# Head statistics by token in 24 columns, preparation reordered, affine parts folded, in the two preparations and two output norms of an RWKV-7 scan

## The reference, cut to what matters

```python
def rwkv7_prepare(pa, prm):
    ...
    decay = jnp.exp(-jnp.exp(-jax.nn.softplus(-w_raw) - 0.5))
    iclr = jax.nn.sigmoid(prm['a0'] + jnp.einsum('bsdl,dlc->bsdc', al, prm['a2']))
    kk = (k * prm['k_k']).reshape(bn, s, A_HEADS_2, HEAD_DIM)
    kk = kk / jnp.maximum(jnp.sqrt(jnp.sum(kk * kk, axis=-1, keepdims=True)), 1e-12)
    k_dir = k[:, :, None, :] * (1 + (iclr - 1) * prm['k_a'])

def rwkv7_output(f, y, prm, dtype):
    mu = jnp.mean(y, axis=-1, keepdims=True)
    var = jnp.mean(jnp.square(y - mu), axis=-1, keepdims=True)
    yn = ((y - mu) * lax.rsqrt(var + GN_EPS)).reshape(bn, s, A_WIDTH_2) * prm['gn_w'] + prm['gn_b']
    bonus = jnp.sum(f['r'][:, :, None] * f['k'] * prm['r_k'], axis=(2, 4))
    yn = yn + (bonus[..., None] * f['v']).reshape(bn, s, A_WIDTH_2)
    return (yn * f['g']).astype(dtype)
```

## Time and profile before

| what | value |
|---|---|
| median of three runs | 3805.64 us (3802.0 to 3807.56) |
| the profiled execution, its time and its span | 3803.02 us, 3801.2 us |
| PE busy in the span | 3201.2 us (84%) |
| DVE busy in the span | 2259.3 us (59%) |
| ACT busy in the span | 1296.1 us (34%) |
| first preparation | 1736.7 to 1785.4 us |
| first output norm | 1972.5 to 1999.1 us |
| second preparation | 1999.1 to 2049.9 us |
| second output norm | 2236.7 to 2264.3 us |

### The profile page before, as it was taken

The page is one execution under the profiler, slowest core; times in us unless marked ns, Lnnn a source line. Parts: engine busy times, 40 slices in busy tenths (PEclk is TensorE's granted clock), DMA queues, the critical chain, the costliest instruction groups (busy, mean ns, idle before and its releaser), DMA issues. The chain is left out here.

```text
span 3801.2 us, 62276 instructions
## 1 busy us (share of the span) xinstructions
PE 3201.2 (84%) x26174; PEld 2598.5 (68%) x26174; DVE 2259.3 (59%) x3957; ACT 1296.1 (34%) x2197; POOL 113.6 (3%) x160
## 2 busy tenths in 40 slices
PE   6679998976999958975765757999999799869998
PEld 5568877644887757843753745888787677657787
DVE  7578876686787566766456455454333546663344
ACT  1233334324333342144323325221233326542233
POOL 0000000200000000000101100000000000000000
PEclk9889999998999979988997988999999898989999
DMA  7235562102334212310000012232212232022231
GB/s 292 99 128 177 171 173 105 68 23 61 123 144 141 87 51 108 125 52 28 5 21 21 4 39 98 89 111 100 78 67 89 78 137 87 1 83 89 89 94 67
DMA packets 64423, 342.37 MB, mean 90 GB/s; under 512 B 15248, under 2 KB 16785, under 8 KB 28433
## 3 DMA queue, kind: packets, MB, share of 16 engines
q1 hardware_dynamic: 61904, 330.75, 25.3%
q0 software_dynamic: 2240, 7.64, 0.6%
HBM read 327.58 MB, written 10.79 MB: 89 GB/s over the span
## 5 line engine op out<-in xcount | busy, mean ns | idle before, releaser
L263 DVE TENSOR_TENSOR weight_lo<-weight_ring,weight_hi 128x1024 fp32r<-128x1024 f32 x341 | 418.7, 1229 | 163.7 <-ACT weight_hi L248 158.4
L248 ACT CAST weight_hi<-weight_ring 128x1024 fp32r<-128x1024 f32 x341 | 355.7, 1043 | 152.6 <-PE banks L418 62.8
L416 PE MATMUL banks<-hT_hi.1,weight_hi 128*128 128x512 f32 x864 | 348.8, 404 | 24.0 <-PEq L380 22.8
L418 PE MATMUL banks<-hT_hi.1,weight_lo 128*128 128x512 f32 x864 | 342.8, 397 | 0.0
L417 PE MATMUL banks<-hT_lo.1,weight_hi 128*128 128x512 f32 x864 | 342.8, 397 | 0.0
L416 PEld LDWEIGHTS banks<-hT_hi.1,weight_hi 128*128 128x128 f32 x864 | 164.3, 190 | 64.2 <-issue 26.0
L417 PEld LDWEIGHTS banks<-hT_lo.1,weight_hi 128*128 128x128 f32 x864 | 164.4, 190 | 38.1 <-issue 1.4
L418 PEld LDWEIGHTS banks<-hT_hi.1,weight_lo 128*128 128x128 f32 x864 | 164.0, 190 | 38.5
L416 PE MATMUL banks<-hT_hi.3,weight_hi 128*128 128x512 f32 (+1 forms) x512 | 175.2, 342 | 7.9 <-PEq L380 7.9
L417 PE MATMUL banks<-hT_lo.3,weight_hi 128*128 128x512 f32 (+1 forms) x512 | 174.1, 340 | 0.0
L418 PE MATMUL banks<-hT_hi.3,weight_lo 128*128 128x512 f32 (+1 forms) x512 | 174.0, 340 | 0.0
(11 more groups left out here) (691 smaller groups left out, 7796.2 us busy)
## 6 DMA issues: line engine op xcount, KB each, us to landing
weight_ring<-ff SPq DMA_DIRECT2D x64, 1024.0 KB, 4.8
weight_ring<-ada SPq DMA_DIRECT2D x48, 1024.0 KB, 4.9
weight_ring<-up SPq DMA_DIRECT2D x44, 1024.0 KB, 4.9
weight_ring<-ada_ffn SPq DMA_DIRECT2D x24, 1024.0 KB, 5.0
weight_ring<-down SPq DMA_DIRECT2D x20, 1024.0 KB, 4.8
first_blocks.1<-ada_mix SPq DMA_DIRECT2D x12, 1024.0 KB, 15.7
weight_ring<-ada_mix SPq DMA_DIRECT2D x12, 1024.0 KB, 4.8
weight_ring<-cv_in SPq DMA_DIRECT2D x8, 1024.0 KB, 4.9
```

The costliest lines, as they stand in the source:

```text
L248: self.nc.scalar.copy(hi, raw).then_inc(self.hi_made, 1)
L263: self.nc.vector.tensor_tensor(lo, raw, hi.bitcast(F32), ALU.subtract).then_inc(self.lo_made, 1)
L416: nc.tensor.matmul(out, w_hi, x_hi, start=first, stop=False)
L418: return nc.tensor.matmul(out, w_lo, x_hi, start=False, stop=last)
```

## The change

It does six things. (1) Sums by head are made by token: the squares are the stationary operand in tiles of 128 tokens, and two columns of `head_ones` the moving one, so that the result is 128 tokens by 2 heads, and all six tiles of both `f` fill 24 columns. (2) Root, maximum and reciprocal work on these 24 columns. (3) `spread_to_features` brings the result back to features: 24 products for each half's pair of tiles, each with one column of the result repeated 64 times as stationary operand and the identity as moving one. `kk`, and `y` in the norm, are multiplied by PSUM directly. (4) The first step of `k_dir` moves from DVE to ACT (an Identity with scale and bias per partition). (5) DVE's order in the preparation changes: the running sums come first with the `k_dir` products between them, then the bonus, then `kk`, the reversal and `iclr*kk`. (6) In the norm the affine part and the sum with the bonus become two `scalar_tensor_tensor`, the second of which also multiplies by the gate, with the shift added after the bonus; one instruction a piece falls away. PE's gate products are cut in two, with the spreading between.

```diff
+    def sums_by_token(to, squares):
+        for t in all_tiles:
+            last = nc.tensor.matmul(to[:, 2 * t:2 * t + 2], squares[:, t * P:(t + 1) * P], head_ones[:, 0:P:HD], start=True, stop=True)
+        return last
+    def spread_to_features(banks, by_token):
+        for t in all_tiles:
+            to = banks[t // 4][:, (t % 4) * P:(t % 4 + 1) * P]
+            for h, part in enumerate((slice(0, HD), slice(HD, P))):
+                last = nc.tensor.matmul(to[part], by_token[:, 2 * t + h:2 * t + h + 1].broadcast_to([P, HD]), ident[:], start=True, stop=True)
+        return last
...
@@ prepare_stage, tensor
-                        for s, seg in enumerate(HALVES):
-                            nc.tensor.matmul(ps[2 * f + s][:, 0:seg.stop - seg.start], head_ones[:], tmp[:, f, seg],
-                                             start=True, stop=True).then_inc(kk_mm, 1)
+                        sums_by_token(ps[7][:, f * 2 * TOK_T:(f + 1) * 2 * TOK_T], tmp[:, f, :]).then_inc(kk_sums, 1)
...
+                    pe.wait_ge(kk_inverse, 1)
+                    for f in range(2):
+                        pe.wait_ge(w_sig, 6 + 2 * f)
+                        spread_to_features(ps[2 * f:2 * f + 2], by_token[:, f, :]).then_inc(kk_spread, 1)
@@ prepare_stage, scalar
-                            nc.scalar.activation(tmp[:, f, seg], ps[2 * f + s][:, 0:seg.stop - seg.start], ACT.Sqrt).then_inc(kk_root, 1)
+                    nc.scalar.activation(by_token[:].rearrange("p f n -> p (f n)"), ps[7][:, 0:4 * TOK_T], ACT.Sqrt).then_inc(kk_root, 1)
...
+                        act.wait_ge(a_sig, 2 * i + 2)
+                        nc.scalar.activation(kdir[:, i, :], iclr[:, i, :], ACT.Identity, bias=omka[:, f0 + f:f0 + f + 1],
+                                             scale=col(R_KA, f0 + f)).then_inc(kdir_begun, 1)
@@ prepare_stage, vector
-                        step(nc.vector.tensor_scalar(tmp[:, f, :], tmp[:, f, :], 1e-12, None, ALU.max))
-                        step(nc.vector.reciprocal(tmp[:, f, :], tmp[:, f, :]))
-                        step(nc.vector.tensor_tensor(kk[:, f, :], kk[:, f, :], tmp[:, f, :], ALU.mult))
...
+                    scan(0)
+                    scan(1)
+                    finish_kdir(0)
+                    scan(2)
+                    finish_kdir(1)
+                    scan(3)
...
+                        dve.wait_ge(kk_spread, f + 1)
+                        for s, seg in enumerate(HALVES):
+                            step(nc.vector.tensor_tensor(kk[:, f, seg], kk[:, f, seg], ps[2 * f + s][:, 0:seg.stop - seg.start], ALU.mult))
@@ head_norm_stage, vector
-                        step(nc.vector.reciprocal(inv[:, f, s], inv[:, f, s]))
-                        step(nc.vector.tensor_tensor(y[:, f, s], y[:, f, s], inv[:, f, s], ALU.mult))
-                        step(nc.vector.tensor_scalar(y[:, f, s], y[:, f, s], rcols[:, R_GW + f0 + f:R_GW + f0 + f + 1],
-                                                     rcols[:, R_GB + f0 + f:R_GB + f0 + f + 1], ALU.mult, ALU.add))
-                        step(nc.vector.tensor_tensor(y[:, f, s], y[:, f, s], mixT[:, f0 + f, s], ALU.add))
+                        dve.wait_ge(spread, f + 1)
+                        step(nc.vector.tensor_tensor(y[:, f, s], y[:, f, s], ps[4 + i][:, 0:n], ALU.mult))
+                        step(nc.vector.scalar_tensor_tensor(out=y[:, f, s], in0=y[:, f, s], scalar=rcols[:, R_GW + f0 + f:R_GW + f0 + f + 1],
+                                                            in1=mixT[:, f0 + f, s], op0=ALU.mult, op1=ALU.add))
                         dve.wait_ge(gate_mm, i + 1)
-                        step(nc.vector.tensor_tensor(mixT[:, f0 + f, s], y[:, f, s], ps[i][:, 0:s.stop - s.start], ALU.mult))
+                        nc.vector.scalar_tensor_tensor(out=mixT[:, f0 + f, s], in0=y[:, f, s], scalar=rcols[:, R_GB + f0 + f:R_GB + f0 + f + 1],
+                                                       in1=ps[i][:, 0:n], op0=ALU.add, op1=ALU.mult)
```

More of the change, by code:

```diff
@@ L2384, in _, with scan @@
                     step = Chain(dve, chained)
[L2385 to L2393 removed]
+                    def scan(i):
                         dve.wait_ge(w_sig, 2 * i + 2)
@@ L2396, in _, with finish_kdir @@
                                                      op0=ALU.mult, op1=ALU.add).then_inc(scanned, 1)
+                    def finish_kdir(i):
+                        dve.wait_ge(kdir_begun, i + 1)
+                        step(nc.vector.tensor_tensor(kdir[:, i, :], kdir[:, i, :], k[:, i % 2, :], ALU.mult))
+                    for f in range(2):
+                        nc.vector.tensor_scalar(kk[:, f, :], k[:, f, :], col(R_KK, f0 + f), None, ALU.mult).then_inc(sq_made, 1)
+                    nc.vector.tensor_scalar(omka[:], rcols[:, R_KA:R_KA + 4], -1.0, 1.0, ALU.mult, ALU.add).then_inc(omka_made, 1)
+                    flat_inverse = by_token[:].rearrange("p f n -> p (f n)")
+                    dve.wait_ge(kk_root, 1)
+                    step(nc.vector.tensor_scalar(flat_inverse, flat_inverse, 1e-12, None, ALU.max))
+                    nc.vector.reciprocal(flat_inverse, flat_inverse).then_inc(kk_inverse, 1)
+                    dve.wait_ge(loaded, 48)
+                    scan(0)
[4 more added lines that the diff above has]
+                    scan(3)
                     dve.wait_ge(scanned, 4)
@@ L2399, in _ @@
                     nc.vector.tensor_copy(gam[:, 1, :, :], chunks[:, :, :, CH]).then_inc(tots, 1)
[L2400 to L2409 removed]
+                    dve.wait_ge(kk_sq, 2)
                     for f in range(2):
+                        finish_kdir(2 + f)
                         step(nc.vector.tensor_tensor(tmp2, kdir[:, f, :], kdir[:, 2 + f, :], ALU.add))
@@ L2864, in _ @@
                         nc.scalar.activation(inv[:, f, s], y[:, f, s], ACT.Square).then_inc(squared, 1)
-                    for i, (f, s) in enumerate(jobs):
-                        act.wait_ge(var_ready, i + 1)
-                        nc.scalar.activation(inv[:, f, s], inv[:, f, s], ACT.Sqrt).then_inc(root_ready, 1)
+                    for f in range(2):
+                        act.wait_ge(var_ready, f + 1)
+                        nc.scalar.activation(by_token[:, f, :], by_token[:, f, :], ACT.Sqrt).then_inc(root_ready, 1)
                 @block.vector
@@ L2875, in _ @@
                                                        op0=ALU.mult, op1=ALU.add).then_inc(centred, 1)
-                    for i, (f, s) in enumerate(jobs):
-                        dve.wait_ge(var_mm, i + 1)
-                        nc.vector.tensor_scalar(inv[:, f, s], ps[4 + i][:, 0:s.stop - s.start], 1.0 / HD, GN_EPS, ALU.mult, ALU.add).then_inc(var_ready, 1)
+                    for f in range(2):
+                        dve.wait_ge(var_sums, f + 1)
+                        nc.vector.tensor_scalar(by_token[:, f, :], ps[6 + f][:, 0:2 * TOK_T], 1.0 / HD, GN_EPS, ALU.mult, ALU.add).then_inc(var_ready, 1)
@@ L2879, in _ @@
+                    for f in range(2):
+                        dve.wait_ge(root_ready, f + 1)
+                        nc.vector.reciprocal(by_token[:, f, :], by_token[:, f, :]).then_inc(inv_ready, 1)
                     dve.wait_ge(centred, 4)
                     for i, (f, s) in enumerate(jobs):
-                        dve.wait_ge(root_ready, i + 1)
-                        step(nc.vector.reciprocal(inv[:, f, s], inv[:, f, s]))
-                        step(nc.vector.tensor_tensor(y[:, f, s], y[:, f, s], inv[:, f, s], ALU.mult))
```

66 lines of the change are left out of this document (35 added, 31 removed).

## The result

The changed kernel takes 3764.71 us, the median of four runs (3763.72 to 3768.02), beside 3803.82 us (3798.84 to 3807.56, four runs) of the kernel before on the same chip. The ratio is 0.9893, with a 95% interval of 0.9881 to 0.9905. The forecast was 3765. The profiled execution took 3763.72 us, with a span of 3761.9.

The account below looks back on a forecast made before the run. DVE was taken to set the end of the four changed stages. Gains of 19.2 (norms), 9.6 and 10.4 us (preparations) take 3803.0 to 3763.8; with the median 2.6 higher, 3765 was written; 8 in 10: 3755 to 3780.

Parts of the forecast that it names:

- The sum: Gain over both preparations and both norms: 19.2 + 9.6 + 10.4 = 39.2 us.
- Records of two columns: PE's sums by token, in preparation and norm: one record starts every 0.12 us, 24 records taking 2.9 us at full clock.
- Spreading: PE's return of the statistics to features: a record every 0.054 us, 24 records taking 1.6 us in the norm.
- The second: Rival: two-column records do not overlap, 0.27 us each at full clock: 3779, chance 0.09; spreading's too: 3798, chance 0.04.
- third: Rival: sums and spreading records run alone at half clock in all four stages, 0.48 us each: 3863; chance 0.03.
- fourth rival: Rival: nothing is gained, since something else ends the stages: 3804; chance 0.03.
- The clock rival: Rival: small products may not keep PE busy in the way that raises its clock: 3769 to 3779; chance 0.11.
- first form: Clock rival's milder case: full clock only after as many us of decay and rate products, first round 2 us more: 3769.
- DVE's tail: Preparation, behind the fourth running sum and the copy of totals: DVE waits for nobody and works 16.6 us.
- The round on ACT: Preparation: two pairs of sigmoids and the new Identity (1.04 us) make a round of 3.0 us.
- The norm's wide work: DVE's three instructions a piece in the output norm: 3.6 us for each `f`, 7.2 us in all.
- The affine step's move: Preparation: moving the first step of `k_dir` from DVE to ACT ends it at 38.1 instead of 39.0, worth 0.9 us.

Follow-up runs that it names:

- e11: The changed kernel once more, unaltered, run beside e9 and e10 on one chip; 3764.57 us, ratio 0.9895 to the kernel before.
- e3: The changed kernel with the first step of `k_dir` back on DVE and ACT's Identity gone; 3774.4 us in one run.
- e10: The changed kernel with 128 moving columns in the norm's sums alone; 3765.35 us, ratio 0.9897 to the kernel before.
- e6: The changed kernel with decay and rate products ahead of the head sums in the preparation; 3762.48 us, ratio 0.9886 to the kernel before.
- e9: The changed kernel with e6's order, the norm's spreading ahead of its gate products, and 128 moving columns in the norm's sums; 3751.3 us, ratio 0.9859.

## Why the prediction was right, step by step

- **The sum.** 39.2 us was forecast for the four stages of a profiled execution, and 39.2 was measured (153.7 - 114.5). That is closer than its terms deserve: by stage (preparation, norm, preparation, norm) 9.6, 9.6, 10.4, 9.6 were forecast and 9.7, 8.4, 11.2, 10.0 came, in e11's execution 8.8, 10.0, 10.9, 10.0. By its own terms the median would be 3763.8 + 2.6 = 3766.4 and not 3765. That 3764.71 came within 0.3 us of the number written is luck, since the rest of the span alone varies by 5.7 us between two executions of the kernel.
- **Records of two columns.** Assumed 0.12 us apart at full clock, measured (2.84 - 0.25) / 23 = 0.113, and 0.213 (24 records in 5.28 us, the last taking 0.37) at half. Spreading: assumed 0.054, measured (2.84 - 0.27) / 47 = 0.055. The second, third and fourth rival fall with this.
- **The clock rival came in part.** It was given 0.11 as a case of its own, outside the forecast; in the runs its first form is the rule in the preparations, at a smaller price than its 2 us a stage. The ground that was given against it does not hold as written: the sums have 24 records of weight load and matmul where there were 8, and move 2 columns a record instead of 512 and 256. Full clock came 4.6 us later than before in the first, the first decay pair took 2.91 us and the first sigmoid started 10.1 us after the start instead of 9.5 (10.7 in e11); one gate pair cost 1.3 us more, so that DVE's wide work in the first norm began 10.3 us after the stage's start (9 forecast; 8.7 in the second). What hid it from the sum is that the terms behind were priced too high, DVE's tail in each preparation by 0.6.
- **The round on ACT** measured 2.94 us (1.03 for the Identity, 1.04 assumed), and the fourth sum ended 11.8 us after the first sigmoid, as worked out.
- **DVE's tail** behind it took 16.2 us where 16.8 with the copy were assumed. The norm's wide work took 7.2, as assumed: a `scalar_tensor_tensor` of 512 columns costs 0.75 rather than 0.69, made good because the last instruction of a piece is not chained to the next one, which starts 0.67 us behind it.
- **The affine step's move** was priced at 0.9 us a stage and is worth 1.4 to 1.9 (e3, one run). What was wrong is the kernel it was compared with: there the four running sums were taken as back to back, 6.8 us in all. In e3's second preparation they take 7.7 without the `k_dir` steps between them, since the second still waits 0.8 for ACT.
- **Transfers and waits.** Nothing else ended the stages; the scans behind them took 183.6 to 190.5 us over all profiles, with 187.1 and 186.7 before and 186.8 and 186.1 after.

What stays open: why the clock fell in 10 norms of 16 and not in the other 6 with the same sums. That the width of the sums is the cause is likely and not shown: it rests on counts, 0 of 10 norms in five kernels against 10 of 16, and not on a comparison of times. e10 and e11 differ by nothing that can be measured.

## What to carry to other kernels

Reduce a statistic to one number per token before you take root and reciprocal of it: the reciprocal costs by the column (4953 ns for 768, 222 for 12), and small products bring the result back cheaply. With 128 stationary columns, moving 128 columns cost almost as much as moving 2 (2.94 and 2.84 us for 24 records), and no norm with such wide sums lost the clock, where 10 of 16 with narrow ones did. Compare changed stages by their own length in the trace, with the granted clock beside it, since the untouched rest of a long kernel varies by more than a small edit is worth; and put first in a stage what the longest chain of waits needs, as e6 and e9 show (4 us a preparation by letting the decay products go ahead of the sums).

## What the runs showed of the hardware that was not expected

- A PE that the profile shows busy 2.00 of 2.00 us can fall to 1.2 GHz: in the first norm the granted clock is 0.59 and 0.55 behind 24 records of two moving columns. The Trainium skill ("TensorE: Matmul & The Clock Gate", the HAM clock gate) ties the full rate to activity; here the profile's busy share stood at its full value while the rate fell, so that share does not foretell the clock.
- 24 records of fp32 products with a 128-column stationary operand take 2.84 us with 2 moving columns and 2.94 us with 128.
- One program's span varied by 5.7 us outside the edited stages between two profiled executions (3647.4 and 3653.1), both at a mean granted clock of 0.935.
